# Mixing and attention in one block, each engine running on by itself

## The reference, cut to what matters

```python
h = rmsnorm(x, norm_mix_g);  p = h @ w_in          # latents, RWKV columns, gate logits
o_a = chunk_causal_attention(q, k, v, ...)         # branch A: 8 heads, softmax over visible keys
o_b, wkv_new, shift_new = rwkv7_time_mix(z, ...)   # branch B: delta-rule state, group norm, gate
x = x + sum_n sigmoid(gate_n) * (branch_n @ w_out[n])
x = x + hier_moe(rmsnorm(x))                       # 32 experts, two of one group for each row
```

## Time and profile before

| | before |
|---|---|
| median of 3 runs | 1544.85 us (1543.92 to 1545.82) |
| the profiled execution: own time, span | 1542.08 us, 1540.3 us |
| mean granted clock of PE over the span | 0.976 |
| PE / DVE / ACT / POOL busy | 1440.2 (94%) / 854.1 (55%) / 474.3 (31%) / 153.9 us (10%) |
| last work of PE in mixing, first in attention | up to 835.82, from 842.90 us |
| first work of PE in merge, end of the span | 1025.14, 1540.3 us |

### The profile page before, as it was taken

The page is one execution under the profiler, slowest core; times in us unless marked ns, Lnnn a source line. Parts: engine busy times, 40 slices in busy tenths (PEclk is TensorE's granted clock), DMA queues, the critical chain, the costliest instruction groups (busy, mean ns, idle before and its releaser), DMA issues. The chain is left out here.

```text
span 1540.3 us, 39034 instructions
## 1 busy us (share of the span) xinstructions
PE 1440.2 (94%) x16352; PEld 1001.3 (65%) x16352; DVE 854.1 (55%) x1942; ACT 474.3 (31%) x986; POOL 153.9 (10%) x145
## 2 busy tenths in 40 slices
PE   6999999999899999999998899979998799999994
PEld 5888888875465665566554566644554677777772
DVE  3555555565767887788775666646777123222220
ACT  2222222225334434433421344434553111111110
POOL 0000000000001011101111000000000222333321
PEclk9999999999999999999998999989999899999998
DMA  9522221446232223222114533437955999999962
GB/s 336 200 96 95 95 95 68 144 160 211 63 113 85 86 85 116 74 67 72 50 55 112 126 88 87 109 119 296 347 194 184 315 330 342 343 354 356 346 237 43
DMA packets 101937, 257.62 MB, mean 167 GB/s; under 512 B 35360, under 2 KB 54448, under 8 KB 92432
## 3 DMA queue, kind: packets, MB, share of 16 engines
q1 hardware_dynamic: 94032, 237.95, 45.0%
q0 software_dynamic: 7744, 17.33, 4.8%
HBM read 203.36 MB, written 60.56 MB: 171 GB/s over the span
## 5 line engine op out<-in xcount | busy, mean ns | idle before, releaser
L559 PEld LDWEIGHTS a_ps<-a_hT,a_wz 128*128 128x128 f32 x1792 | 202.6, 192 | 6.1 <-issue 3.8
L559 PE MATMUL a_ps<-a_hT,a_wz 128*128 128x128 f32 x1792 | 204.1, 275 | 1.7 <-DMA a_wz<-w_z 1.7
L2080 PE MATMUL d_ps<-late,last_down 128*128 128x512 f32 x256 | 115.1, 596 | 1.7 <-DVE last_down L1828 1.0
L2461 DVE TENSOR_SCALAR f_y<-f_down,table 96x512 f32<-96x512 f32 x32 | 23.9, 747 | 119.3 <-PE f_down L2255 73.6
L2262 DVE COPY f_xT<-f_turned 128x384 f32<-128x384 f32 x32 | 17.8, 558 | 125.1 <-PE f_turned L2229 122.5
L2080 PEld LDWEIGHTS d_ps<-late,last_down 128*128 128x128 f32 x256 | 46.6, 190 | 51.1 <-issue 49.7
L1586 ACT ACTIVATE late<-c_score,c_top 128x1024 f32<-128x1024 f32 (+8 forms) x72 | 50.5, 702 | 92.3 <-DVE c_top L1535 91.8
L1222 PE MATMUL b_ps<-b_wg,r_hT 128*128 128x512 f32 x128 | 65.8, 637 | 0.4 <-DMA r_hT<-hT_d 0.4
L2468 ACT ACTIVATE f_xT<-f_turned 128x384 f32<-128x384 f32 x32 | 15.7, 490 | 162.7 <-PE f_turned L2229 159.3
L1008 DVE STREAM_TRANSPOSE b_U<-b_T 64x256 f32<-64x256 f32 x144 | 63.3, 439 | 2.7
L906 DVE TENSOR_TENSOR b_M<-b_ps,r_causal 128x512 f32<-128x512 f32 x72 | 46.3, 685 | 32.8 <-PE b_ps L1285 32.8
(11 more groups left out here) (381 smaller groups left out, 2831.1 us busy)
## 6 DMA issues: line engine op xcount, KB each, us to landing
wgu<-w_gate_up SPq DMA_DIRECT2D x15, 2048.0 KB
late<-w_gate_up SPq DMA_DIRECT2D x9, 2048.0 KB
wd<-w_down SPq DMA_DIRECT2D x17, 1024.0 KB
late<-w_down SPq DMA_DIRECT2D x10, 1024.0 KB
r_hT<-hT_d SPq DMA_DIRECT2D x16, 512.0 KB, 4.3
b_hT<-hT_d SPq DMA_DIRECT2D x16, 512.0 KB, 3.9
gate_d<-b_logits SPq DMA_DIRECT2D x32, 256.0 KB, 4.1
late<-gate_d SPq DMA_DIRECT2D x8, 1024.0 KB, 6.6
```

The costliest lines, as they stand in the source:

```text
L559: mm = pe.matmul(banks[Z_BANKS[n % 2]][:, j * P:(j + 1) * P], wz[:, i, (g + j) * P:(g + j + 1) * P], hT[t % 2][:, i, :], start=(i == 0), s ...
L2080: mm = pe.matmul(banks[2 + u][:], oT[t % 2][:, HB * branch(u) + k, :], wo[:, HB * branch(u) + k, half(u)], start=(k == 0), stop=(k == HB - 1))
```

## The change

Attention no longer has a block of its own: it gets the one of inputs and mixing, which closes after attention. What the block's end had ordered is now ordered by single waits.

- PE waits for mixing's banks by name: for `y_copied` and `state_out` ahead of the first scores in banks 2 and 3, and for `gram_copied` and `logits_copied` ahead of the first `turn`.
- DVE's `finish(LAST)` is handed to attention and stands between `maximum(0, 0)` and `maximum(0, 1)`.
- SP's last stores of mixing, with the waits for their landing, are handed over as `last_stores`, and stand behind the load of the identity and ahead of head 1's load.
- POOL waits for head 0's first output store before it clears mixing's semaphores.
- The SBUF tiles `normed`, `qT1`, `kT1`, `v1` and `out1` take other places in the order of allocation.

```diff
--- before.py
+++ after.py
@@ -685,9 +685,9 @@
         X = sb("X", [P, RD])
         W = sb("W", [P, RD])
         S = [sb(f"S{j}", [P, PAIRS, P]) for j in range(2)]
+        normed = sb("normed", [P, RD])
         grown = sb("grown", [P, PAIRS, P])
         y = sb("y", [P, H, RH])
-        normed = sb("normed", [P, RD])
         bonus = sb("bonus", [P, RD])
         st = sb("st", [P, 2, H])
         (set_done, lora_in, kk_sq, lora_done, gate_done, gate_copied, kk_ready, w_sig, a_sig, nn_ready, nn_root,
@@ -705,6 +705,21 @@
         consts_in = early["consts_in"]
         next_ones = hand_over()
         CONSTS = 11
+        late = dict(y_copied=(y_copied, NT), state_out=(state_out, 2), gram_copied=(gram_copied, PAIRS * NT),
+                    logits_copied=(logits_copied, ITEMS), sems=sems)
+
+        def last_stores(sp):
+            sp.wait_ge(out_ready, NT)
+            sp.dma_start(io["ob_d"][LAST], y[:]).then_inc(ob_stored, 16)
+            sp.wait_ge(state_out, 2)
+            sp.dma_start(io["wkv"][1], grown[:]).then_inc(state_stored, 16)
+            sp.wait_ge(state_stored, 32)
+            sp.wait_ge(ob_stored, 16 * NT)
+            for j in range(2):
+                sp.wait_ge(logits_stored[j], stores_upto(ITEMS + j))
+            sp.wait_ge(no_logits, 32)
+
+        late["stores"] = last_stores
 
         def after(eng, sem, n):
 
@@ -798,15 +813,6 @@
                 if s == LAST:
                     sp.wait_ge(state_out, 1)
                     sp.dma_start(io["wkv"][0], grown[:]).then_inc(state_stored, 16)
-            sp.wait_ge(out_ready, NT)
-            sp.dma_start(io["ob_d"][LAST], y[:]).then_inc(ob_stored, 16)
-            sp.wait_ge(state_out, 2)
-            sp.dma_start(io["wkv"][1], grown[:]).then_inc(state_stored, 16)
-            sp.wait_ge(state_stored, 32)
-            sp.wait_ge(ob_stored, 16 * NT)
-            for j in range(2):
-                sp.wait_ge(logits_stored[j], stores_upto(ITEMS + j))
-            sp.wait_ge(no_logits, 32)
 
         @block.gpsimd
         def _(pool):
@@ -1039,7 +1045,7 @@
                             next_state(t)
                 if there(n):
                     start_T(n)
-            finish(LAST)
+            late["last_output"] = lambda: finish(LAST)
 
         @block.scalar
         def _(act):
@@ -1419,7 +1425,7 @@
                             bonus_factors(n)
                         if k >= 8:
                             products(n, k - 8)
-    return sems
+    return late
 
 
 def load_head(sp, io, early, h, j, sem):
@@ -1429,7 +1435,7 @@
     sp.dma_start(early["v"][j], head(io["v_d"]).rearrange("t p o n -> p t (o n)")).then_inc(sem, 16)
 
 
-def attention(nc, io, keep, early, signals, used):
+def attention(nc, io, keep, early, signals, late, block):
     STEPS = NT
     with ExitStack() as c:
         sb = lambda n, s: c.enter_context(nc.sbuf_tensor("c_" + n, s, F32))
@@ -1439,14 +1445,15 @@
         turned = [ps(f"turned{i}", [P, 512]) for i in range(3)]
         acc = ps("acc", [P, 512])
         ident = sb("ident", [P, P])
-        qT, kT, v = early["qT"], early["kT"], early["v"]
-        qT[1], kT[1], v[1] = sb("qT1", [QK, NT, P])[:], sb("kT1", [QK, NT + 1, P])[:], sb("v1", [P, NT + 1, VD])[:]
         probs = [keep["gate"][1].rearrange("p a b -> p (a b)")[:, i * NPT * P:(i + 1) * NPT * P] for i in range(2)]
         probsT = [keep["o"][1].rearrange("p a (b c) -> p (a b) c", c=P), sb("probsT1", [P, NPT, P])]
         top = sb("top", [P, 2])
         total = sb("total", [P, 3])
         inv = sb("inv", [P, 1])
-        out = [sb(f"out{j}", [P, NT, VD]) for j in range(2)]
+        out = [sb("out0", [P, NT, VD])]
+        qT, kT, v = early["qT"], early["kT"], early["v"]
+        qT[1], kT[1], v[1] = sb("qT1", [QK, NT, P])[:], sb("kT1", [QK, NT + 1, P])[:], sb("v1", [P, NT + 1, VD])[:]
+        out.append(sb("out1", [P, NT, VD]))
         (const_in, score_done, score_free, top_ready, exp_done, turn_done, turn_dve, turn_act, pv_done, acc_copied,
          total_free, dve_step) = (sem(n) for n in (
              "const_in score_done score_free top_ready exp_done turn_done turn_dve turn_act pv_done acc_copied "
@@ -1455,7 +1462,6 @@
         HEAD_START = (0, START)
         out_stored = [sem("out_stored0"), sem("out_stored1")]
         begun = keep["begun"]
-        block = c.enter_context(nc.Block())
 
         keys = [[(k, P) for k in range(i + 1)] for i in range(NPT)] + [[(PAST_TILE, P), (NPT, DEC)]]
         width = [sum(n for _, n in ks) for ks in keys]
@@ -1502,6 +1508,7 @@
                         load(u + 1, j)
 
             sp.dma_start(ident[:], io["ident"]).then_inc(const_in, 16)
+            late["stores"](sp)
             load(0, 1)
 
             for dst, src in ((begun["ident"][:], io["ident"]), (begun["wr"][:], io["w_router"]), (begun["br"][:], io["b_router"].partition_broadcast(P)),
@@ -1519,7 +1526,8 @@
 
         @block.gpsimd
         def _(pool):
-            give_back(pool, used)
+            pool.wait_ge(out_stored[0], 16 + START)
+            give_back(pool, late["sems"])
 
         @block.vector
         def _(dve):
@@ -1565,6 +1573,7 @@
                     dve.tensor_scalar(out[j][:, s, :], acc[:, 0:VD], inv[:, 0:1], None, ALU.mult).then_inc(acc_copied, 1)
 
             maximum(0, 0)
+            late["last_output"]()
             maximum(0, 1)
             step.lap()
             copy_turned(0, 0)
@@ -1657,8 +1666,12 @@
 
             pe.sem_inc(pv_done, 1)
             scores(0, 0)
+            pe.wait_ge(*late["y_copied"])
+            pe.wait_ge(*late["state_out"])
             scores(0, 1)
             pe.wait_ge(const_in, 16 + START)
+            pe.wait_ge(*late["gram_copied"])
+            pe.wait_ge(*late["logits_copied"])
             turn(0, 0)
             scores(0, 2)
             rounds(pe, body)
@@ -2539,10 +2552,10 @@
             ahead["weights_in"] = signal(c, "", [f"{w}_in{j}" for w, n in (("up", WB_UP), ("down", WB)) for j in range(n)])
             return [*ahead["attention"].values(), *ahead["weights_in"].values()]
 
-        with ExitStack() as first_stages:
-            block = first_stages.enter_context(nc.Block())
-            inputs = inputs_stage(nc, io, early, in_inputs, block)
-            used_in_mixing = mixing(nc, io, early, in_mixing, inputs, hand_over, block)
+        first_stages = c.enter_context(ExitStack())
+        block = first_stages.enter_context(nc.Block())
+        inputs = inputs_stage(nc, io, early, in_inputs, block)
+        late_in_mixing = mixing(nc, io, early, in_mixing, inputs, hand_over, block)
         upto_mixing.close()
         keep = dict(
             run=sb("run", [P, NE]),
@@ -2573,7 +2586,8 @@
                 ("x0", [D]))}
             keep["begun"].update(ident=keep["ident"], gate0=keep["gate"][0], o0=keep["o"][0])
             keep["begun_in"] = {n: upto_merge.enter_context(nc.semaphore("m_" + n)) for n in ("consts", "gate", "x", "o")}
-            attention(nc, io, keep, early, ahead["attention"], used_in_mixing)
+            attention(nc, io, keep, early, ahead["attention"], late_in_mixing, block)
+            first_stages.close()
             upto_attention.close()
             in_mixing.close()
             last_up, last_down = (c.enter_context(nc.sbuf_tensor(n, [P, k], F32, side="right")) for n, k in (("last_up", up_size), ("last_down", 2 * D)))
```

## The result

| | before | changed |
|---|---|---|
| median | 1544.85 us (5 runs, 1540.43 to 1548.42) | 1532.55 us (5 runs, 1531.04 to 1534.37) |
| ratio to before | | 0.9921, 95% interval 0.9905 to 0.9937 |
| profiled execution, its span | 1542.08, 1540.3 us | 1531.04, 1529.2 us |
| PE's last work of mixing ends | 835.82 us | 833.23 us |
| from there to the first scores / to the third maximum | 7.08 / 18.05 us | 0.36 / 7.82 us |

The kernel is 12.3 us faster by its medians (9.7 to 14.7 us by the interval). The table splits the traces' difference: 10.2 us between PE's last work of mixing and the third maximum (18.05 - 7.82), 2.6 us ahead of the joint, where the change has no part, and 1.7 us the other way behind it (0.1 in attention, the rest from merge on).

What follows compares the result with a forecast made beforehand. PE was taken as the bound, idling 7.08 us before attention for mixing's stores, with a lowered clock after. Gains up to the third maximum came to 9.7 us, other terms 0: 1544.85 - 9.7 = 1535.1 us, range 1532.8 to 1539.3.

Steps and rivals of the forecast that it cites:

- The bound at the joint: Between mixing and attention: PE idles 7.08 us while SP waits for mixing's stores to land, which PE needs none of.
- Start of the scores: Attention's first scores on PE start at 836.45 instead of 842.90 us, 6.45 us gained, with 0.2 us allowed for semaphores.
- First maximum: DVE's first maximum in attention: corner masked at 838.42 instead of 846.74 us, 8.32 us gained; maximum ends at 839.79.
- Turn: PE's first turn in attention, behind the first exponential, starts at 841.17 us and takes 1.09 us at full clock.
- The moved finish: DVE's finish of mixing's last tile, between the first two maxima: takes 3.10 us but costs only 0.3 on the path.
- Third maximum: DVE's `maximum(0, 2)` in attention begins at 844.15 instead of 853.87 us, 9.72 us gained.
- Waits added to PE: PE's new waits ahead of the first scores and first turn cost only their issue, taken as 0.
- Identity and head 1's load: SP's loads in attention: identity lands at 839.8, wanted at 841.17; head 1's v has 4.7 us reserve; cost 0.
- The sum of 9.7 us: Total gain forecast from PE's end in mixing to `maximum(0, 2)`, carried unchanged to the end of the kernel.
- The rest moves as a whole: Behind `maximum(0, 2)`, the rest of attention, merge and experts keep their old distances and end 9.7 us earlier.
- Clock at 1.00 from 820 to 860 us: Sign expected in the changed kernel's profile: PE's granted clock stays at full level from mixing's end into attention.
- The first rival: PE's clock falls in its new 2.4 us pause before the first turn, costing 3 us: 1538.1 us; chance 0.14.

Runs made afterwards that it cites:

- the filled hold: Changed kernel with PE held until mixing's last stores land, DVE's finish before the first maximum, seven extra matmuls in the hold; ratio to the kernel before 0.9978.

## Why the prediction was wrong

**Point by point.** *The bound at the joint*, right: PE's hole was the landing of stores that nothing near needs, and with PE held for them the gain is gone. *Start of the scores*: 0.63 us forecast, 0.36 measured; the 0.2 for semaphores was too much, since the trace has PE start at 833.59, within ACT's root (833.48 to 833.68), so ACT's release, which stands behind the root in its program, came before the root's end. *First maximum*: 2.60 us behind PE's last work of mixing forecast, 2.39 measured. *Turn*: 5.35 forecast, 5.15 measured. *The moved finish*: 3.10 us, and DVE the bound up to the third maximum; right, with the scores 0.1 us ahead of it instead of 0.3. *Third maximum*: 8.33 forecast, 7.82 measured. The sum of 9.7 us stands beside 10.2, 9.1 and 8.2 us in three traces, and 9.5 us between the medians of all runs. *Waits added to PE*, nothing: right. *Identity and head 1's load*, covered: right, with 4.0 instead of 4.7 us of reserve. *The rest moves as a whole*: right for attention (171.4 us from the third maximum to merge, 171.3 before); from the start of merge to the end of the span 1.5 us went the other way in this pair of traces. Over all twelve traces this part takes 515.2 to 520.8 us, and the first trace of before has the lowest of them; what makes that scatter is not shown here. *Clock at 1.00 from 820 to 860 us*: so in the first trace, not in the other two.

**The step that failed** is the last one, from the sum to the time: "The median shown lies 2.77 us above the profiled one, a distance that I keep", and with it the width, "Other executions shift the clock's falls ... by some microsecond either way ... spreads the forecast to about 1533 to 1537". I took three runs within 1.9 us for the scatter of the kernel. Over 77 runs it was 14.5 us, with a median of 1543.90, 0.95 below my base; from that base the forecast is 1534.2, and the 23 runs of the changed kernel have a median of 1534.37. The first five of them gave 1532.55, the two later series 1532.1 and 1535.51. So the mechanism and the size of the joint held, and the median that the range was drawn for fell out of it by the scatter of a few runs, for which the range had too small a term. That it fell 0.25 us out and not in is chance, and so is the unbroken clock of the first trace, one of three.

**The first rival was mis-sized.** I gave the fall of the clock in the new pause a chance of 0.14 and a price of 3 us. It came in two of the three traces of the changed kernel and costs 1.2 and 2.1 us. The kernel with head 1's load late, the same program up to the third maximum, has it too (third maximum 9.31 us behind PE's last work of mixing, 1.5 more than without the fall). The argument against it, that both falls before had followed longer idling, was weak: behind the same pause of 2.62 us the clock was at 1.00 once and fell to 0.50 twice. The rule that stood beside it, that the same idle stretch falls at another phase each time (the Trainium skill, "TensorE: Matmul & The Clock Gate", section "Part 1: The HAM clock gate"), agrees with these traces, which don't show the phase itself. The three microseconds were too much since I had the turn at the lower clock as well: it took 1.06 us in all three traces, and only the scores behind it were slow, by 1.19 and 0.99 us, nearly all of which the third maximum waited for.

## What to carry to other kernels

Where a block ends, ask of each engine which of the awaited things it needs itself: here PE needed banks that were free, and waited 7 us for stores to land; and count the clock that falls in such a gap, 2.5 us by the filled hold. What is moved past the joint must be looked at in the order of every engine that it passes: filling PE's pause gave nothing until ACT's release was taken out from behind a root. And when the gain is below 1%, take the joint's own duration from several traces, and the scatter of the total from many runs, before a range is drawn around a sum.

## What the runs showed of the hardware

- PE's clock fell behind two pauses of only 0.73 and 0.55 us (between 436 and 440 us in the first trace of before, clock 0.50 from 440 to 443), and not behind the same stretch of work in the changed kernel's first trace (clock 1.00).
- Behind a pause of the same 2.62 us PE's clock stayed at 1.00 once and fell twice, among three traces of one kernel; in the third of them it was at 0.50 for all of 841 to 846 us.
- The load of one head's v (320 KB) landed after 6.2 and 7.2 us on a nearly empty queue, and after 10.6 and 10.9 us behind or beside other transfers (head 0's at 808 us, and head 1's behind merge's constants).
- Executions of one kernel differ by up to 0.9% (1536.05 to 1550.56 us over 77), and PE's last work of mixing ends up to 3 us apart from trace to trace in programs that are the same up to there.
